# Moving TensorE's input tiles by 32 bytes in each SBUF partition, and everything behind them by 128

## The reference

```python
def first_block(x, c, ...):
    mod = silu(c) @ w_ada + b_ada                        # six vectors of 1024
    h = x * (1 + sc1) + sh1
    y = hybrid_mixer(h, ...)                             # h @ w_in, SSD scan, attention, @ w_out
    x = layer_norm(ALPHA * x + (1 + g1) * y, ...)
    h = x * (1 + sc2) + sh2
    ff = square(relu(h @ w_ff_in)) @ w_ff_out            # 1024 -> 4096 -> 1024
    return layer_norm(ALPHA * x + (1 + g2) * ff, ...)

def second_block(x, mem, ...):
    for i in range(2):
        x = x + 0.5 * swiglu_ffn(rms_norm(x), w1_in[i], w1_out[i])    # 1024 -> 2 x 2816 -> 1024
        x = x + (pool_mixer if i == 0 else nsa_mixer)(rms_norm(x), ...)
        x = x + memory_cross_attention(rms_norm(x), rms_norm(mem), ...)
        x = x + 0.5 * swiglu_ffn(rms_norm(x), w2_in[i], w2_out[i])
    return rms_norm(x)
```

## The kernel before, in words

| tile | first byte | remainder by 128 |
|---|---|---|
| `raw`/`w_lo` 0 to 3, then `w_hi` 0 to 3, 8192 bytes each | 16512 to 73856 | 0 |
| `X` | 82048 | 0 |
| `x_hi`, `x_lo`, 8192 each | 90240, 98432 | 0 |
| `memN`, `par` | 106624, 114816 | 0 |
| `ident`, `ones_d`, masks | 117792 and on | 32 |
| `work_space` (12 KB, shared by `gu`, `sg`, `hb`, `Pr`, `PT` and others) | 132640 | 32 |
| `arena` (80 KB, shared by `hid_hi`, `hid_lo`, `T8`, `mh`, `ml`, `qT`, `V` and others at whole KB in it) | 144928 | 32 |

## Time and profile before

### The profile page before, as it was taken

How to read it: one execution, slowest core, us unless ns; L and a number is a source line. 1 busy time by engine, 2 the same in 40 slices (tenths; PEclk the granted TensorE clock), 3 DMA queues, 4 the chain that set the end, 5 groups by cost and what they waited for, 6 DMA issues and landing times.

```text
span 1645.8 us, 31707 instructions
## 1 busy us (share of the span) xinstructions
PE 1599.7 (97%) x12998; PEld 1570.2 (95%) x12998; DVE 1062.9 (65%) x1557; ACT 840.3 (51%) x1209; POOL 170.8 (10%) x223
## 2 busy tenths in 40 slices
PE   7999999999999999999999999999999999999998
PEld 7999989999999999999999999999998889999998
DVE  7687877876555766575666556655655776566653
ACT  5565556655445444454544444444465555454442
POOL 2013200400113400010000000000100111000000
PEclk9899999999999999999999999999999999999999
DMA  9562963365553554562554465545654014255453
GB/s 390 202 227 85 369 244 149 135 242 187 185 179 133 204 181 156 181 226 102 176 183 171 161 208 182 186 160 181 222 187 152 27 58 174 103 179 179 170 173 117
DMA packets 45125, 293.14 MB, mean 178 GB/s; under 512 B 5200, under 2 KB 6496, under 8 KB 15712
## 3 DMA queue, kind: packets, MB, share of 16 engines
q1 hardware_dynamic: 41184, 265.49, 45.6%
q0 software_dynamic: 3840, 26.23, 4.1%
HBM read 288.02 MB, written 3.67 MB: 177 GB/s over the span
## 4 chain that ended last, share of the span: by engine, by line
PE 79%; DVE 11%; ACT 5%; DMA 4%; issue 1%; DVEq 0%; POOL 0%; SPq 0%; POOLq 0%; ACTq 0%
PE G L447 24%; PE G L449 23%; PE G L448 23%; DVE w_lo L1598 4%; PE O L638 3%; ACT w_hi L1056 2%; DMA mod_x<-w_ada 2%; PE L L1017 1%; PE T L624 1%; DMA mod_w<-w_ada 1%; PE L L886 1%; DVE mod_x L1565 1%; DVE X L1724 1%; DVE XB L1868 1%; ACT x_hi L1133 1%
## 5 line engine op out<-in xcount | busy, mean ns | idle before, releaser
L1598 DVE TENSOR_TENSOR w_lo<-raw,w_hi 128x2048 fp32r<-128x2048 f32 (+1 forms) x256 | 540.6, 2115 | 210.6 <-ACT w_hi L1056 210.1
L447 PE MATMUL G<-x_hi,w_hi 128*128 128x256 f32 x2176 | 622.5, 286 | 6.0 <-DVE w_lo L1598 4.6
L448 PE MATMUL G<-x_lo,w_hi 128*128 128x256 f32 x2176 | 618.7, 284 | 0.0
L449 PE MATMUL G<-x_hi,w_lo 128*128 128x256 f32 x2176 | 618.6, 284 | 0.0
L1056 ACT ACTIVATE w_hi<-raw 128x2048 fp32r<-128x2048 f32 (+1 forms) x260 | 458.0, 1765 | 155.0 <-DMA raw<-w_ffout 37.7
L447 PEld LDWEIGHTS G<-x_hi,w_hi 128*128 128x128 f32 x2176 | 420.3, 193 | 9.2 <-DVE w_lo L1598 6.2
L448 PEld LDWEIGHTS G<-x_lo,w_hi 128*128 128x128 f32 x2176 | 420.2, 193 | 0.1
L449 PEld LDWEIGHTS G<-x_hi,w_lo 128*128 128x128 f32 x2176 | 420.0, 193 | 0.0
L447 PE MATMUL G<-hid_hi,w_hi 128*128 128x256 f32 x1280 | 362.9, 284 | 2.2 <-DVE hid_lo L1630 2.1
L449 PE MATMUL G<-hid_hi,w_lo 128*128 128x256 f32 x1280 | 359.0, 280 | 0.0
L448 PE MATMUL G<-hid_lo,w_hi 128*128 128x256 f32 x1280 | 358.9, 280 | 0.0
(11 more groups left out here) (411 smaller groups left out, 1825.6 us busy)
## 6 DMA issues: line engine op xcount, KB each, us to landing
raw<-w_f1in SPq DMA_DIRECT2D x44, 1024.0 KB, 4.8
raw<-w_f2in SPq DMA_DIRECT2D x44, 1024.0 KB, 4.8
raw<-w_f1out SPq DMA_DIRECT2D x32, 704.0 KB, 4.1
raw<-w_f2out SPq DMA_DIRECT2D x32, 704.0 KB, 4.1
raw<-w_ffin SPq DMA_DIRECT2D x16, 1024.0 KB, 4.8
raw<-w_ffout SPq DMA_DIRECT2D x16, 1024.0 KB, 4.8
mod_x<-w_ada POOLq DMA_DIRECT2D x12, 1024.0 KB, 7.3
mod_w<-w_ada POOLq DMA_DIRECT2D x8, 1024.0 KB, 13.5
```

What stands on the lines that cost most here:

```text
L447: mm(out, l_hi, r_hi, start=start, stop=False)
L448: mm(out, l_hi, r_lo, start=False, stop=False)
L449: return mm(out, l_lo, r_hi, start=False, stop=stop)
L1598: v.tensor_tensor(w_lo[b][:, 0:s.size], raw[b][:, 0:s.size], w_hi[b][:, 0:s.size].bitcast(F32), ALU.subtract).then_inc(s_lo, 1)
```

## The change

Two tiles that nothing reads or writes are declared: 32 bytes ahead of `x_hi`, and 96 bytes behind `x_lo`.

```diff
         X = sb("X", [P, KC, S])
+        sb("ahead_of_x", [P, 8])
         x_hi = sb("x_hi", [P, KC, S], F32R)
         x_lo = sb("x_lo", [P, KC, S], F32R)
+        sb("behind_x", [P, 24])
         memN = sb("memN", [P, KC, S])
```

## The result

The changed kernel took 1632.91 us in the median of four runs (1632.64 to 1636.16), the kernel before 1650.65 us in four beside them (1648.32 to 1652.45). The ratio is 0.9897, with a 95% interval of 0.9884 to 0.9911: 17 us, 1.0%, less. The forecast was 1637.

The account below looks back on a forecast made before the run. PE's matmul pace was taken as the bound. Savings of 13.5 + 0.8 = 14.3 us took the profiled 1647.55 to 1633.3; the median's 3.55 us above it made 1637, with an 80% range of 1633 to 1648.

Parts of the forecast that it names:

- PE's pace is what counts, and it goes with the place of the tile: Whole kernel: PE is busy 97% of the span, and tiles at remainder 0 by 128 bytes run slowest, 120.0 ns.
- the rival that goes with this: Input matmuls: the pace isn't made by the address, or remainder 32 alone doesn't help; 1651 us, chance 0.12.
- I take it that it gets hid's paces too: Input tiles, 32 bytes on: 2.3 ns less per matmul, 13.5 us over the 5856 on the path.
- the sum: Whole kernel: 13.5 us from input matmuls on the path plus 0.8 us from early ones, 14.3 us saved.
- I take 128, so hid keeps its pace: Hid matmuls: only the distance's remainder by 128 counts, so 0 us; 8.8 us if the gain were lost.
- the slower case: Input and hid matmuls: repeat after 256 or 512 bytes, one common pace; loses from 119.15 ns, 1660 us at 120; chance 0.05.
- The early 672 matmuls: Input matmuls before 230 us: 1.5 us whole, none if the modulation holds the path; half taken, 0.8 us.
- `gemm_b`: Matmuls with x stationary, 224 x 3: gain taken as 0, 1.8 us if worth the full 2.7 ns.
- The 118.1 ns of the mixer's output: Hid stretch at 288 us, 12.28/104: pace counted for 384 of hid's matmuls, 1.9 ns each against 120.0.
- the forecast's own range: Whole kernel: 1633.5 us with every x stretch at 117.3 ns, to 1643 with every one at 118.6; chance 0.75.
- A stretch keeps the pace with which it began.: Hid stretches: several steady paces, 117.2 to 120.0 ns, each stretch keeping its first; x has only the slowest.

Follow-up runs that it names:

- The region alone: Against the kernel before: input tiles where they were, everything behind them 128 bytes on; 1650.76 us, ratio 1.0003.

## Why the prediction was right, and where not

**Right: PE's pace is what counts, and it goes with the place of the tile.** The input tiles left 120.0 ns and the time fell by nearly as much as the sum of their matmuls; DVE and ACT delivered. By the Trainium skill, TensorE: Matmul & The Clock Gate, "Step-by-step: what each phase is for", loading the next weights takes nothing from the running matmul. The prediction gave the rival that goes with this, no gain and 1651 us, a chance of 0.12. The runs here differ from it: an operand's distance moved the time by up to 2.4%. Whether it is the ports, the banks behind them or the load's order no run here tells.

**Mis-sized: "I take it that it gets hid's paces too", 2.3 ns.** The input tiles got 116.7 and 117.8, 3.1 ns less than before in the mean. Hid's paces of before belong to a distance of 160, the changed kernel's distance is 32. With 2.3 ns, the sum was 14.3 us; the median fell by 17.7, the ratio says 17.0 (14.7 to 19.1). The kernel with the input tiles at 160 is what that step described. In its trace four of the five long input streams ran at 117.3 and one at 118.6; over all input matmuls after 230 us the single starts give 117.7, which is 2.3 ns below 120.0, just as counted:

```profile
342.00:408.00 66.00, 66.00 (x565) 1.00 0.60 216
565.00:640.00 75.00, 75.00 (x642) 1.00 0.49 173
1457.00:1560.00 103.00, 103.00 (x880) 1.00 0.51 178
```

Yet this execution took only 8.8 us less than the profiled one before, and the median of ten runs 7.8 us less.

**Left out: what the clock and the waits take back.** Some 3 us of what is missing in the trace with 160 bytes are the clock's (0.990 of 1637.0 us there, 0.992 of 1645.8 before). In the profiled pair above, the clock and the waits took 6 of 21.7 us. The sum had nothing for either, and nothing for hid's own gain of 3.5 us. So part of the nearness of 1637 to 1633 is luck: two gains too small, 4.7 us by the input tiles' pace and 3.5 by hid's, stood against losses that were left out.

**Wrong: "I take 128, so hid keeps its pace".** The repeat is 256 bytes, which I had left open between 128, 256 and 512 and put under the slower case. Hid did change sets, from 160's to 32's. The premise of that rival came true and its price didn't: at a distance of 32 the common pace is 116.7 to 117.8, below the 119.15 from which the change would have lost. The region alone is worth nothing that could be measured (1.0003), in a trace in which hid's long stretches had drawn 117.8; in the changed kernel's they had drawn 116.7, the 3.5 us above.

**The early 672 matmuls and `gemm_b`.** These were small terms (0.8 us and 0). `gemm_b` went from 120.0 to 118.3 ns; taking 0 for it was off by about a microsecond, as 672 matmuls by 1.7 ns. The row that the prediction went by, `mh` as the stationary tile, could not show this gain: the distance there is 96, and the pace by the single starts 120.0 as well.

**Two readings.** The mean durations of the matmuls with x moving are 284 to 286 ns in the earlier trace rows, and 283 is `gemm_b`'s. The 118.1 ns of the mixer's output, from a stretch of only 12 us, is 118.67 by the single starts; this makes the 2.3 ns 2.2. The upper end of the forecast's own range, 1643, is 1642 by its own sum.

**"A stretch keeps the pace with which it began."** Seen again in every kernel. Of the streams without a pause of over 135 ns none that is 96 matmuls or longer, up to 1007, changes its pace after its first 15 matmuls. What a stream draws at its start stays open: the same kernel with the input tiles at 192 ran at 1620 and at 1636 us. Nothing tried here steers it, except that the distance sets what there is to draw.

## What to carry to other kernels

In a stream of matmuls that each load new weights, compare stretches by their pace before anything else: length over count, for each pair of operand tiles. Two values for the same shape, clock and feed can be a sign that the place of the operands costs time, and a tile of a few dozen bytes that nobody uses can test it. Test several distances: here 32 bytes gave 1.0%, 96 gave nothing, and 192 for both kinds of moving tile 2.4%. Shift only one group of tiles in each test, or two effects hide in one edit.

## What was not expected of the hardware

- The time from one float32r matmul of 256 columns to the next depends on the distance from the stationary to the moving operand in the partition, between 113.3 and 120.0 ns, and not on either address (all tiles 32 bytes on: ratio 0.9998).
- It repeats with 256 bytes (32 and 288; 160 and 416), isn't monotonic in between, and the sign counts (96: 120.0 ns, 160: 117.3 or 118.6, in `gemm_a` and in `gemm_b`).
- For most distances there are two steady paces, and a stream of a thousand matmuls keeps the one it has: 117.9 and 116.6 in two streams of one execution. In the traces here a stream of 96 or more changed its pace only after a pause.
